# Index projections in a fused attention step: a fifth tile's first feature half placed ahead, the remaining projections one step ahead of the transposes

## The chip, the core and the metric

The kernel runs on one core of a Trainium2 chip. The metric is the device time of one execution in microseconds (us), as a median of several executions. TensorE (PE in the profile) does the matrix products, VectorE (DVE) and ScalarE (ACT) work on tensors, GpSimd (POOL) helps with elementwise work, and SyncE (SP) issues most of the transfers. Each engine takes its own instructions in the order in which they are written; semaphores are the only thing that orders one engine against another.

## The reference, cut to what matters

One layer of a streaming encoder is computed for 1024 prompt tokens and 64 sample tokens, width 1024. The input is normed and modulated to `h`, one combined projection gives everything else, and two attention branches (one that picks its keys by an indexer, one with a sliding window) are gated, merged and added to the input. The part that the change touches is the indexer: its queries `i_q` (4 heads of 64), its key `i_k` (64) and its head weights `i_w` (4), together 324 columns of `h @ w_in`, and the scores made from them.

```python
h = rmsnorm(x, norm_g) * (1 + scale) + shift
p = dict(zip(COL_NAMES, jnp.split(h @ w_in, offs, axis=-1)))
dots = jnp.einsum('nqhd,nkd->nqhk', iq.astype(f32), ik.astype(f32)) * IDX_DIM ** -0.5
score = jnp.einsum('nqhk,nqh->nqk', jax.nn.relu(dots), iw.astype(f32)) * IDX_HEADS ** -0.5
_, sel = lax.top_k(score, k_sel)
```

## The kernel before, in words

The tokens lie in NT = 9 tiles: eight of 128 prompt tokens and one, SAMPLE = 8, of 64. Products in full precision are made from a rounded value and its remainder: `three` issues high times high, high times low and low times high. `HH` and `HL` are the high and low parts of the transposed `h`, 8 blocks of 128 features each; `WH` and `WL` are those of one chunk of the weights.

`project(i, f)` multiplies tile i by the index weights over the feature blocks 4f to 4f+3, that is 12 matmuls of 324 columns, into the PSUM bank `ibank(i)`. Both halves of a tile add up in one bank. Tiles 0 to 3 have banks 0, 1, 4 and 5, and all later tiles have bank 0, so that project(i, 0) of a later tile has to wait (on `idx_evac`) until ScalarE has copied the tile before it out of that bank. `hl_done` counts the parts of `HL` that VectorE has finished. These come in the order of `HORDER`: the first feature half for tokens 0 to 127, 128 to 511 and the rest, then the second feature half in the same three parts.

The first halves of tiles 0 to 3 stand between the last products of the modulation (`ada`). Then comes a loop over i from 0 to ITEMS = 13 in which every engine takes its part:

- TensorE: the projections, then the transposes of item j = i - 1 (L1716, six of them, waiting on `idx_lo`), then the scores of tile j (L1656) for j from 2 to 7, with a piece of the next weight chunk in quarters among the heads. Pieces are the other columns of the combined projection, one tile by 512 columns, 24 matmuls. Piece p is issued at i = p + NAT0, NAT0 = 4. Pieces 0 to 4 all have bank 1 (`pbank`), so piece p waits on `piece_ev` for piece p - 1 to be read out.
- ScalarE: first `nat_evac` of the piece of the iteration before (a copy at L1086 and eight squares with a sum at L1093), then `idx_out(i)`, which copies the projection of tile i to `NIDX` (L1047) and raises `idx_evac`, then the copies of the transposes of item i - 1 to `IQT` (L1117) and `IKT` (L1124), then the relus of the scores (L1078).
- VectorE: `idx_high(i)` makes the rounded part of tile i, then the scores of tile i - 1 are summed up.
- GpSimd: the remainders (L890, L896), which raise `idx_lo`, and for i below 4 one low part of the next chunk's weights (L876).
- SyncE: waits on `idx_evac` for tile i and stores its `i_k` rows (L650, `ik_out`), and for i below 4 a load of raw weights. `NIDX` has two slots, so `idx_out(i)` waits for `ik_out` of tile i - 2, counted on one of two semaphores, and for `idx_lo` of i - 1 items.

After this loop TensorE goes on with the pieces of all remaining chunks, then the attention, then the output projections.

Of the kernel before, what the change touches and what calls it, by code (L numbers as in the profile page):

```python
# [31 lines left out]
NT = SEQ // 128 + 1  # L32
# [15 lines left out]
def rows_of(t):  # L48
    return DEC if t == SAMPLE else 128
# [12 lines left out]
def build_program(nc, t):  # L62

    ctx = ExitStack()
    with ctx:
# [3 lines left out]
        def sem(name):  # L69
            return ctx.enter_context(nc.semaphore(name))  # L70
# [4 lines left out]
        def bank(b):  # L75
            return PS[:, b, :]
# [181 lines left out]
        mod_ready = sem("mod_ready")  # L258
# [9 lines left out]
        idx_evac = sem("idx_evac")  # L268
# [91 lines left out]
        def tcols(tt):  # L360
            return slice(128 * tt, 128 * tt + rows_of(tt))
# [20 lines left out]
        NAT0 = 4  # L382
# [4 lines left out]

        def ibank(i):

            return (0, 1, 4, 5)[i] if i < NAT0 else 0  # L390

        def pbank(p):

# [88 lines left out]
        for q, (_, x) in enumerate(TQ):  # L482
            if x[0] == "P" and unit_keys(x[1]) > 512:
                EV.append("SV"[x[2]])
            else:
                EV.append("V" if EV.count("V") <= EV.count("S") else "S")
# [521 lines left out]
        def _(act):  # L1008
            def w_hi(n):

                c, k = n // KD, n % KD
                if c >= NCH:
                    return
                cw = CHUNKS[c][2]
                if c:
                    act.wait_ge(raw_in[n % 4], 16 * (n // 4 - 1))
                else:
                    act.wait_ge(iraw_in[k // 4], 16)
                if k == 0 and c == 2:
                    act.wait_ge(idx_pe, NT)  # L1020
                if k == 0 and c >= 3:
                    act.wait_ge(piece_pe, PEND[c - 2])
                nc.scalar.activation(WH[c % 2][:, k, 0:cw], RAW[:, n % 4, 0:cw] if c else IRAW[:, k, :], ACT.Copy).then_inc(hi_done, 1)  # L1023
# [16 lines left out]
            def idx_out(i):  # L1040

                r = rows_of(i)
                act.wait_ge(idx_pe, i + 1)
                if i >= 2:
                    act.wait_ge(ik_out[i % 2], 16 * (i // 2))
                    act.wait_ge(idx_lo, i - 1)
                nc.scalar.activation(NIDX[0:r, i % 2, :], bank(ibank(i))[0:r, 0:IDX_W], ACT.Copy).then_inc(idx_evac, 1)  # L1047
# [24 lines left out]
            def relus(tt):  # L1072
                for h in range(4):
                    n = SHEADS.index((tt, h))
                    r, nk = rows_of(tt), keys_of(tt)
                    act.wait_ge(score_pe, n + 1)
                    v = PS[0:r, 4 + 2 * (n % 2):6 + 2 * (n % 2), :].rearrange("p b n -> p (b n)")[:, 0:nk]
                    nc.scalar.activation(v, v, ACT.Relu, scale=HD ** -0.5 * 0.5).then_inc(relu_done, 1)  # L1078

            def nat_evac(c, j, p):  # L1080

                r = rows_of(j)
                dst = STG2[0:r, p % 2, :] if c == 1 else STG[0:r, STG_Q[p] % 3, :]
                if c == 1 and p >= 2:
                    act.wait_ge(stg2_out[p % 2], 16 * (p // 2))
                nc.scalar.activation(dst, bank(pbank(p))[0:r, :], ACT.Copy).then_inc(nat_copied, 1)  # L1086
                act.wait_ge(nat_copied, p + 1)
                blocks = [b for b in range(8) if (8 * (c - 1) + b) % 12 < 10]
                for b in blocks:
                    f = 8 * (c - 1) + b  # L1090
                    head = 10 * (f // 12) + f % 12
                    v = bank(pbank(p))[0:r, HD * b:HD * (b + 1)]
                    last = nc.scalar.activation(v, v, ACT.Square, accum_out=SSQ[0:r, 20 * j + head:20 * j + head + 1])  # L1093
                last.then_inc(piece_ev, 1)

            for i in range(ITEMS + 1):
                if 0 <= i - 1 - NAT0 < NT:
                    act.wait_ge(piece_pe, i - NAT0)
                    nat_evac(1, i - 1 - NAT0, i - 1 - NAT0)
                if 1 <= i < NT:  # L1100
                    idx_out(i)
                if NT <= i < ITEMS:
                    act.wait_ge(idx_t, i - 1)
                    act.wait_ge(cik_in, 16)
                    nc.scalar.activation(IN2[i % 2][:, 4, 0, :], CIK[:, i - NT, :], ACT.Copy)
                    nc.scalar.activation(IN2[i % 2][:, 4, 1, :], CIK[:, i - NT, :], ACT.Copy).then_inc(idx_hi, 1)
                if NT <= i < ITEMS:
                    for n in range(2):
                        w_hi(2 * KD + 2 * (i - NT) + n)
                if i >= 1:  # L1110
                    j = i - 1
                    r = rows_of(j) if j < NT else 128
                    act.wait_ge(idx_t, j + 1)
                    if j == 0:
                        act.wait_ge(hl_done, 24)
                    if j < NT:
                        nc.scalar.activation(IQT[:, :, tcols(j)], bank(2).rearrange("p (h n) -> p h n", h=4)[:, :, 0:r], ACT.Copy)  # L1117
                    if j < SAMPLE:
                        dst = IKT[:, :, tcols(j)]
                    elif j == SAMPLE:  # L1120
                        dst = IKTS[:, :, PAST:PAST + DEC]
                    else:
                        dst = IKTS[:, :, 128 * (j - NT):128 * (j - NT + 1)]
                    nc.scalar.activation(dst, bank(3)[:, 0:256].rearrange("p (h n) -> p h n", h=2)[:, :, 0:r], ACT.Copy).then_inc(idx_tev, 1)  # L1124
                    if 2 <= j < SAMPLE:
                        relus(j)
# [55 lines left out]
            for s in range(S0, S1):  # L1182
# [56 lines left out]
                if s in CACHE_STEP:  # L1239
                    i = CACHE_STEP[s]  # L1240
# [313 lines left out]
        def _(pe):  # L1554
            T = nc.tensor

            def three(out, wh, wl, mh, ml, first, last):

                T.matmul(out, wh, mh, start=first, stop=False)  # L1559
                T.matmul(out, wh, ml, start=False, stop=False)  # L1560
                return T.matmul(out, wl, mh, start=False, stop=last)  # L1561
# [18 lines left out]
            def project(i, f):  # L1580

                r = rows_of(i)
                part = [q for q in range(3) if PARTS[q][1] >= 128 * i + r][0]
                pe.wait_ge(lo_done, 4 * (f + 1))
                pe.wait_ge(hl_done, 12 * f + 4 * part + 4)
                if i >= NAT0:
                    pe.wait_ge(idx_evac, 1 if i == NAT0 else i)
                for k in range(4 * f, 4 * f + 4):
                    last = three(bank(ibank(i))[0:r, 0:IDX_W], HH[:, k, tcols(i)], HL[:, k, tcols(i)],
                                 WH[0][:, k, 0:IDX_W], WL[0][:, k, 0:IDX_W], k == 0, k == KD - 1)  # L1590
                if f == 1:
                    last.then_inc(idx_pe, 1)
# [45 lines left out]
            for i in range(NAT0):  # L1638
                ada(1, 2 * i)
                ada(1, 2 * i + 1)  # L1640
                if i == NAT0 - 1:
                    mod_transposes(1)
                project(i, 0)

            def score_head(tt, h):

# [48 lines left out]
                        piece(p, [h])  # L1695

            for i in range(ITEMS + 1):
                if i == 0:
                    project(0, 1)
                if i + 1 < NAT0:  # L1700
                    project(i + 1, 1)
                if NAT0 <= i < NT:
                    project(i, 0)
                    project(i, 1)
                if i >= 1:
                    j = i - 1
                    r = rows_of(j) if j < NT else 128
                    pe.wait_ge(idx_lo, j + 1)
                    if j >= 1:
                        pe.wait_ge(idx_tev, j)  # L1710
                    slot = IN2[j % 2]
                    for h in range(6):
                        if h < 4 and j >= NT:
                            continue
                        dst = bank(2)[:, 128 * h:128 * h + r] if h < 4 else bank(3)[:, 128 * (h - 4):128 * (h - 4) + r]
                        last = T.transpose(dst.bitcast(F32R), slot[0:r, h, :, :].rearrange("p a d -> p (a d)"), IDR[0:r, 0:r])  # L1716
                    last.then_inc(idx_t, 1)
                    p = i - NAT0 if 0 <= i - NAT0 < NT else None
                    if j == 2:
                        pe.wait_ge(idx_evac, NAT0)  # L1720
                    if 2 <= j < SAMPLE:
                        score(j, p)
                    elif p is not None:
                        piece(p)
# [197 lines left out]
```

## Time and profile before

| what | value |
|---|---|
| median of 3 executions | 1015.71 us (1014.78 to 1016.16) |
| the profiled execution | 1014.79 us |
| its span, first to last instruction | 1013.0 us |
| mean granted clock of TensorE, share of full speed | 0.979 |
| TensorE busy | 953.0 us |
| VectorE busy | 653.4 us |
| ScalarE busy | 393.9 us |
| GpSimd busy | 375.7 us |

In the views a time is in microseconds from the start of the span. In a timeline row the first number is the start of the first instruction of the row, the second how long the row lasted, and what stands in brackets is the idle time of the engine before it with what ended it. A matmul's duration is longer than the distance to the next one, since matmuls overlap; the step from start to start is what a stream of them costs. PEclk is the granted clock, 1.00 for 2.4 GHz and 0.50 for 1.2 GHz.

### The profile page before, as it was taken

The page shows a single profiled execution, that of the slowest core. Times are in us where ns is not written, and L with a number is a line of the kernel's source. Part 1 is how long each engine was busy: PE and PEld are TensorE (multiplying, and loading weights), DVE is VectorE, ACT ScalarE, POOL GpSimd, SP SyncE. Part 2 cuts the span into 40 slices and gives each one's busy share as a digit, 9 for nine tenths or more (in the row PEclk, how much of TensorE's full clock was granted, in tenths as well). Part 3 has the DMA queues.
Part 4 walks back from the last instruction along what each step waited for, and adds up shares of the span by engine and source line. Part 5 has one row for each costly group of instructions (what it writes and reads, how often), then busy time and mean ns, then how long its engine had stood idle before and what let it go on. Part 6 is the DMA issues. An engine that isn't in the chain of part 4 may idle for free.

```text
span 1013.0 us, 17631 instructions
## 1 busy us (share of the span) xinstructions
PE 953.0 (94%) x6468; PEld 851.8 (84%) x6482; DVE 653.4 (65%) x1375; ACT 393.9 (39%) x1166; POOL 375.7 (37%) x420
## 2 busy tenths in 40 slices
PE   3859999999999999999999889999999879999998
PEld 2558887878789999999999767778867769999998
DVE  6563365999999999999980477665665543331111
ACT  5674566444322322122211566666655522212100
POOL 0261123222243533121233488655640325527332
PEclk9989999999999999999999799999999989999999
DMA  9830013643461323232132755433246475534242
GB/s 322 304 78 25 24 46 107 225 154 102 140 202 60 115 82 108 80 108 76 63 136 70 236 147 145 122 92 86 83 129 174 108 232 152 153 98 135 97 124 73
DMA packets 113243, 126.92 MB, mean 125 GB/s; under 512 B 13161, under 2 KB 90361, under 8 KB 113034
## 3 DMA queue, kind: packets, MB, share of 16 engines
q1 hardware_dynamic: 102754, 114.82, 36.5%
q10 hardware_dynamic: 10408, 11.01, 3.5%
q8 instruction: 52, 0.85, 0.4%
q14 instruction: 29, 0.24, 0.1%
HBM read 95.75 MB, written 36.02 MB: 130 GB/s over the span
## 4 chain that ended last, share of the span: by engine, by line
PE 81%; issue 5%; POOL 4%; DVE 3%; ACT 3%; DMA 3%; SPq 1%; ACTq 0%; POOLq 0%; DVEq 0%
PE PS L1559 20%; PE PS L1560 20%; PE PS L1561 20%; PE PS L1801 6%; PE PS L1827 5%; PE PS L1742 4%; PE PS L1656 2%; PE PS L1760 1%; PE PS L1805 1%; POOL YO L1004 1%; PE PS L1620 1%; DMA XN<-in_x_prompt 1%; DMA ZST<-attd 1%; PE PS L1568 1%; DVE HL L1338 1%
## 5 line engine op out<-in xcount | busy, mean ns | idle before, releaser
L1559 PE MATMUL PS<-HH,WH 128*128 128x384 f32 (+1 forms) x576 | 188.8, 328 | 0.0
L1561 PE MATMUL PS<-HH,WL 128*128 128x384 f32 (+1 forms) x576 | 187.9, 326 | 0.0
L1560 PE MATMUL PS<-HL,WH 128*128 128x384 f32 (+1 forms) x576 | 187.7, 326 | 0.0
L1394 DVE MAX8 M<-SC 128x8 f32<-128x384 f32 (+3 forms) x210 | 174.7, 870 | 11.6 <-DVE SC L1399 11.0
L1399 DVE MATCH_REPLACE8 SC<-M,SC 128x384 f32<-128x384 f32 (+3 forms) x210 | 179.9, 863 | 0.0
L876 POOL TENSOR_TENSOR WL<-RAW,WH 128x512 fp32r<-128x512 f32 x72 | 94.2, 1312 | 180.8 <-ACT WH L1023 180.8
L1559 PE MATMUL PS<-WH,HH 128*128 128x512 f32 (+3 forms) x288 | 110.2, 382 | 8.9 <-DVE HL L1338 8.7
L1559 PEld LDWEIGHTS PS<-HH,WH 128*128 128x128 f32 x576 | 108.1, 188 | 3.8 <-issue 3.7
L1560 PE MATMUL PS<-WL,HH 128*128 128x512 f32 (+3 forms) x288 | 108.3, 376 | 0.0
L1561 PE MATMUL PS<-WH,HL 128*128 128x512 f32 (+3 forms) x288 | 108.2, 376 | 0.0
L1560 PEld LDWEIGHTS PS<-HL,WH 128*128 128x128 f32 x576 | 108.1, 188 | 0.0
L1561 PEld LDWEIGHTS PS<-HH,WL 128*128 128x128 f32 x576 | 108.1, 188 | 0.0
L1221 ACT ACTIVATE PB<-PB,NM 128x256 f32<-128x256 f32 (+9 forms) x136 | 86.2, 634 | 25.1 <-DVE NM L1495 24.0
L1150 ACT ACTIVATE STG<-PS 128x384 f32<-128x384 f32 (+1 forms) x48 | 22.8, 475 | 155.1 <-PE PS L1561 155.1
L1559 PE MATMUL PS<-UH,MH 128*128 128x256 f32 (+1 forms) x288 | 81.5, 283 | 0.0
L1560 PE MATMUL PS<-UL,MH 128*128 128x256 f32 (+1 forms) x288 | 81.4, 283 | 0.0
L1561 PE MATMUL PS<-UH,ML 128*128 128x256 f32 (+1 forms) x288 | 81.2, 282 | 0.0
L1559 PE MATMUL PS<-ZH,WOH 128*128 128x384 f32 (+1 forms) x192 | 63.9, 333 | 9.0 <-DVE TM L1538 5.7
L1549 DVE TENSOR_TENSOR YT<-PS,GATE 128x256 f32<-128x256 f32 (+1 forms) x36 | 15.3, 424 | 87.0 <-PE PS L1561 71.2
L1559 PEld LDWEIGHTS PS<-WH,HH 128*128 128x128 f32 (+1 forms) x288 | 53.8, 187 | 20.0 <-POOL WL L876 8.8
L1495 DVE CUSTOM_DVE_ANT_0 PB<-PS,BTA 128x256 f32<-128x256 f32 (+6 forms) x56 | 46.1, 823 | 33.5 <-PE PS L1805 21.9
L1742 PE MATMUL PS<-IDF,PB 128*128 128x128 f32 (+1 forms) x436 | 65.4, 279 | 0.1
(202 smaller groups left out, 1957.0 us busy)
## 6 DMA issues: line engine op xcount, KB each, us to landing
RAW<-in_w_all SPq DMA_DIRECT2D x72, 256.0 KB, 2.7
gz<-STG SPq DMA_DIRECT2D x48, 192.0 KB, 1.8
WADA<-in_w_ada SPq DMA_DIRECT2D x16, 512.0 KB, 11.9
snat<-STG SPq DMA_DIRECT2D x24, 256.0 KB, 2.0
QKV<-snat SPq DMA_DIRECT2D x8, 768.0 KB, 5.8
GT<-gz SPq DMA_DIRECT2D x32, 192.0 KB, 2.5
XN<-in_x_prompt SPq DMA_DIRECT2D x8, 512.0 KB, 6.6
btad<-bvd ACTq DMA_DIRECT2D x4, 1024.0 KB
```

Of the source, the lines that this page charges most:

```text
L876: nc.gpsimd.tensor_tensor(WL[c % 2][:, k, 0:cw], raw, WH[c % 2][:, k, 0:cw].bitcast(F32), ALU.subtract).then_inc(lo_done, 1)
L1150: nc.scalar.activation(STG[:, q % 3, 0:gn], bank(pbank(p))[:, 0:gn], ACT.Sigmoid).then_inc(piece_ev, 1)
L1221: nc.scalar.activation(PB[u % NPB][0:r, 0:nk], PB[u % NPB][0:r, 0:nk], ACT.Exp, scale=-1.0, bias=NM[0:r, br, h:h + 1], accum_out=DEN[0:r, ...
L1394: V.max(M8[0:r, a, :], w).then_inc(sel_step, 1)
L1399: V.match_replace(w, M8[0:r, a, :], w, TAKEN).then_inc(sel_step, 1)
L1495: V.tensor_tensor_reduce(out=PB[u % NPB][0:r, 0:nk], in0=v, in1=bias, scale=1.0, scalar=init, op0=ALU.add, op1=ALU.min, accum_out=NM[0:r, ...
L1559: T.matmul(out, wh, mh, start=first, stop=False)
L1560: T.matmul(out, wh, ml, start=False, stop=False)
L1561: return T.matmul(out, wl, mh, start=False, stop=last)
L1742: last = T.transpose(out[0:m, c:c + r], PB[v % NPB][0:r, 128 * b:128 * b + m], IDF[0:r, 0:r])
L1801: last = T.matmul(out, q, keys[:, kv, part, k0 + b:k0 + b + m], start=(part == 0), stop=(part == 1 and br == 1))
L1827: last = T.matmul(PS[half, 7, 128 * h:128 * h + r], v, PT[PSLOT[u + kv] % 3][0:m, p_col(u + kv, b):p_col(u + kv, b) + r], start=(b == 0), ...
```

## The change

Tile 4 gets a bank of its own, bank 6. Its first feature half is issued right after that of tile 3, before the loop; its second half is issued in the loop at i = 2. The second halves of tiles 1, 2 and 3 are spread otherwise (0 and 1 at i = 0, 2 and 3 at i = 1). Tiles 5 to 8, which were projected at the iteration of their own number, are now projected one iteration earlier, at i = 4 to 7, so that there is no projection at i = 8. ScalarE copies tile 4 out at i = 3, after tile 3; the others keep their places on ScalarE. The first score waits for five copies rather than four. No instruction is added or removed.

```diff
         def ibank(i):
 
-            return (0, 1, 4, 5)[i] if i < NAT0 else 0
+            return (0, 1, 4, 5, 6)[i] if i <= NAT0 else 0
...
-                if 1 <= i < NT:
+                if 1 <= i < NT and i != NAT0:
                     idx_out(i)
+                if i == NAT0 - 1:
+                    idx_out(NAT0)
...
                 pe.wait_ge(hl_done, 12 * f + 4 * part + 4)
-                if i >= NAT0:
-                    pe.wait_ge(idx_evac, 1 if i == NAT0 else i)
+                if i == NAT0:
+                    pe.wait_ge(mod_ready, 1)
+                if i > NAT0 and f == 0:
+                    pe.wait_ge(idx_evac, 1 if i == NAT0 + 1 else i)
...
                 project(i, 0)
+            project(NAT0, 0)
...
-                if i == 0:
-                    project(0, 1)
-                if i + 1 < NAT0:
-                    project(i + 1, 1)
-                if NAT0 <= i < NT:
-                    project(i, 0)
-                    project(i, 1)
+                for n in {0: (0, 1), 1: (2, 3), 2: (4,)}.get(i, ()):
+                    project(n, 1)
+                if NAT0 <= i < NT - 1:
+                    project(i + 1, 0)
+                    project(i + 1, 1)
...
                     if j == 2:
-                        pe.wait_ge(idx_evac, NAT0)
+                        pe.wait_ge(idx_evac, NAT0 + 1)
```

## Rows read from the trace of the kernel before

**Rows 1.** The page: chain that ended last, by engine.
```profile
PE 81%; issue 5%; POOL 4%; DVE 3%; ACT 3%; DMA 3%; SPq 1%; ACTq 0%; POOLq 0%; DVEq 0%
```
**Rows 2.** Busy time by stretch (busy us and instructions of each engine, PEclk, DMA).
```profile
45.00:84.00 39.00, 27.30 (x170) 23.65 (x169) 22.49 (x46) 23.16 (x52) 20.48 (x25) 0.82 0.25 62
84.00:145.00 61.00, 60.85 (x325) 52.04 (x324) 24.42 (x41) 32.97 (x121) 6.36 (x16) 1.00 0.07 25
145.00:560.00 415.00, 414.09 (x2357) 382.23 (x2356) 363.82 (x660) 125.33 (x479) 127.01 (x118) 1.00 0.35 114
```
**Rows 3.** Timeline of TensorE, 52 to 83 us: projections, transposes (L1716), first scores.
```profile
52.95 0.38 PE L1559 MATMUL PS<-WH,HH 128*128 128x324 f32 x1 [0.90 <-DVE HL L1338]
...
59.34 0.46 PE L1559 MATMUL PS<-WH,HH 128*128 128x324 f32 x1 [4.37 <-DVE HL L1338]
...
69.66 0.96 PE L1716 MATMUL PS<-IDR,IN 128*128 128x128 f32 x6 [2.69 <-POOL IN L896]
72.18 1.00 PE L1716 MATMUL PS<-IDR,IN 128*128 128x128 f32 x6 [1.56 <-POOL IN L896]
74.24 1.62 PE L1656 MATMUL PS<-IKT,IQT 128*128 128x384 f32 x4 [1.05 <-ACT IKT L1124]
...
77.98 0.47 PE L1559 MATMUL PS<-WH,HH 128*128 128x324 f32 x1
...
82.47 0.63 PE L1716 MATMUL PS<-IDR,IN 128*128 128x128 f32 x6
```
**Rows 4.** Timeline of VectorE: the last `HL`, all of `hl_done`.
```profile
66.86 0.76 DVE L1338 TENSOR_TENSOR HL<-XT,HH 128x576 fp32r<-128x576 f32 x1 [0.34 <-ACT HH L1068]
```
**Rows 5.** Timeline of ScalarE, 71 to 74 us: tile 3 out, then the transposes' copies.
```profile
71.41 0.45 ACT L1047 ACTIVATE NIDX<-PS 128x324 f32<-128x324 f32 x1
73.22 0.60 ACT L1117 ACTIVATE IQT<-PS 128x512 fp32r<-128x512 f32 x1 [1.36 <-PE PS L1716]
73.72 0.38 ACT L1124 ACTIVATE IKT<-PS 128x256 fp32r<-128x256 f32 x1
```
**Rows 6.** SyncE, 70 to 80 us: tile 2's store issued; landing times of both stores there.
```profile
71.29 0.43 SPq L650 DMA_DIRECT2D out_pa_ik<-NIDX  x1
...
DMA to landing us min/median/max: 2.6/2.6/2.6
```
**Rows 7.** Timeline of TensorE, end of piece 0, tile 5's projection, transposes, piece 1.
```profile
90.07 0.39 PE L1561 MATMUL PS<-WH,HL 128*128 128x512 f32 x1
90.30 0.31 PE L1559 MATMUL PS<-WH,HH 128*128 128x324 f32 x1
...
93.88 0.62 PE L1716 MATMUL PS<-IDR,IN 128*128 128x128 f32 x6
94.34 0.47 PE L1559 MATMUL PS<-WH,HH 128*128 128x512 f32 x1
```
**Rows 8.** Timeline of ScalarE beside it: piece 0 read out (8 squares), then tile 5.
```profile
90.50 0.60 ACT L1086 ACTIVATE STG<-PS 128x512 f32<-128x512 f32 x1 [0.78 <-PE PS L1561]
...
92.67 0.21 ACT L1093 ACTIVATION_READ_ACCUMULATOR PS<-PS 128x1 f32 x1
94.08 0.44 ACT L1047 ACTIVATE NIDX<-PS 128x324 f32<-128x324 f32 x1 [1.20 <-PE PS L1561]
```
**Rows 9.** Timeline of TensorE at i = 8: tile 8's projection (24 matmuls), transposes.
```profile
128.38 0.31 PE L1559 MATMUL PS<-WH,HH 128*64 128x324 f32 x1
...
131.91 0.63 PE L1716 MATMUL PS<-IDR,IN 128*128 128x128 f32 x6
```
**Rows 10.** Timeline of ScalarE at i = 8: the copy of piece 3.
```profile
128.58 0.60 ACT L1086 ACTIVATE STG<-PS 128x512 f32<-128x512 f32 x1 [0.48 <-PE PS L1561]
```
**Rows 11.** Busy time by stretch of 1 us, around the falls and rises of the clock, and one long wait.
```profile
59.00:60.00 1.00, 0.66 (x3) 0.69 (x4) 1.00 (x2) 0.03 (x1) 1.00 (x1) 0.76 0.67 158
...
69.00:70.00 1.00, 0.34 (x3) 0.35 (x4) 0.74 (x3) 0.00 (x0) 1.00 (x4) 0.88 0.00 0
...
585.00:586.00 1.00, 0.00 (x0) 0.00 (x0) 1.00 (x3) 0.73 (x3) 1.00 (x1) 1.00 0.04 11
```

## The prediction

> **What bounds the kernel now.** First I read the chain that ended last: 81% of it is TensorE [rows 1]. Then I cut the span into stretches. From 84 to 145 us, the part of the loop that has pieces, TensorE is busy for 60.85 of 61 us, and from 145 to 560 us for 414.09 of 415 [rows 2]. The reader is to see that there is no slack on TensorE from 84 us on: whatever TensorE loses or saves there moves the end by the same amount. Before 84 us it is otherwise: 27.30 of 39 us are busy, at a mean clock of 0.82 [rows 2]. The timeline of TensorE shows the holes: 0.90 and 4.37 us in wait for the low parts of `h`, 2.69 and 1.56 us in wait for GpSimd's remainders, 1.05 us in wait for ScalarE's copies [rows 3]. Last I read ScalarE's timeline around one full iteration of the loop, since two of its copies decide when PSUM banks 0 and 1 are free.
>
> **The change part by part.** The matmuls are the same ones; only their places and waits differ.
>
> *Tile 4's first half ahead.* It is 12 matmuls. A projection at full clock takes 93.88 - 90.30 = 3.58 us for 24 [rows 7], so half of one is 1.8 us. Tile 3's first half ends where the hole of 0.90 us begins, at 52.05, so this one ends at about 53.9. It waits for the third part of `HL`'s first half, which VectorE makes before the part that project(0, 1) waits for at 52.95, and for the modulation, older still. It pushes project(0, 1), 12 matmuls, from 52.95 to about 53.9, and that ends near 55.7 instead of 54.8. Behind it lies the hole of 4.37 us that VectorE ends at 59.34 [rows 3]. Cost 0; if that hole were not there, 1.8.
>
> *Second halves regrouped, tile 4's at i = 2.* project(3, 1) now goes ahead of the transposes of item 0, which therefore end near 66.9 rather than 65.0. ScalarE and VectorE are at work on the last part of `h` until 67.6 [rows 4], and their copies come after it, so nobody waits. project(4, 1) needs the last `HL`, done at 66.86 + 0.76 = 67.62 [rows 4]. It runs to about 69.5, and the next transposes start at 69.66, when GpSimd lets them [rows 3]. It just fits in the hole of 2.69 us. Cost 0; at half clock it would run 1.5 us over, but the transposes behind are bound by GpSimd again at 72.18, so that this too would be hidden.
>
> *ScalarE copies tile 4 at i = 3.* This copy has a new neighbour: it stands ahead of the copies of item 2's transposes, and it waits for the store of tile 2's keys, since both use the same slot of `NIDX`. SyncE issues that store at 71.29, behind its load of raw weights, and the landing takes 2.6 us [rows 6], so 73.89; the copy takes 0.45 [rows 5], so 74.3. In the kernel before, the copies behind it start at 73.22 [rows 5], and the first score at 74.24 waits for them [rows 3]. What is queued behind the waiting copy is `IQT` and `IKT`, and who waits for those is TensorE. Cost +1.1 us. If the store landed before 72.8 it would be 0; these are the two bounds.
>
> *Tile 5 in place of tile 4 at i = 4.* Same place, same 24 matmuls, bank 0 long free. Cost 0. It took 82.47 - 77.98 = 4.5 us because its first part ran at half clock [rows 3].
>
> *Tiles 6, 7, 8 at i = 5, 6, 7.* Here is the term that decides. Before, the projection of tile i at iteration i needed the copy of tile i - 1, done an iteration ago. Now iteration 5 opens with project(6, 0), and that needs the copy of tile 5. ScalarE makes this copy at its own iteration 5, but behind `nat_evac` of piece 0, and piece 0 is what TensorE has only just ended. So TensorE's stream stops. The working from the rows: the last matmul of piece 0 starts at 90.07 and the next instruction at 90.30 [rows 7]; ScalarE starts the copy of the piece at 90.50, and ends the last of the eight squares at 92.88 [rows 8]. The copy of tile 5 would follow with some 0.1 us of overlap, as neighbours on ScalarE have, and 0.44 long [rows 8]: 92.76 to 93.2. From the end of a copy on ScalarE to TensorE's start goes 0.14 us (`IKT` ends 74.10, the score starts 74.24) [rows 3, 5]. So project(6, 0) starts at 93.34 instead of 90.30: a stall of 3.04 us. Before, the projection covered this reading out: it and the transposes fill 90.30 to 94.34 [rows 7], and piece 1 finds its bank free. Tiles 7 and 8 have the same stall. Cost 3 x 3.04 = +9.1 us. Bounds: 2.9 to 3.2 each.
>
> *Iteration 8 without a projection.* The 24 matmuls of tile 8 took 131.91 - 128.38 = 3.53 us [rows 9]; these go. But they covered the reading out of piece 3, which begins at 128.58 [rows 10]. Now the transposes (0.46 us, as 94.34 - 93.88 [rows 7]) come first, and piece 4 waits for its bank 1 until 2.38 + 0.20 + 0.14 = 2.72 us after the end of piece 3. That leaves 2.26 us idle. Cost -3.53 + 2.26 = -1.3 us. ScalarE's copies for the first head come before the piece's first quarter is over, so the score doesn't wait further.
>
> *The sum at the clock of before.* 0 + 0 + 1.1 + 0 + 9.1 - 1.3 = +8.9 us.
>
> **The clock.** After the 4.37 us wait the granted clock goes to half within 59 to 60 us; after the 2.69 us wait at about 69.8 [rows 3, 11]. But at 585 us a wait of over 2 us leaves it at 1.00 [rows 11]. My stalls of 3.04 us lie between, so a fall after one of them can go either way. What one costs: 24 matmuls took 4.5 us where they began at half clock against 3.58 at full [rows 3, 7], that is 0.9, and as 12 matmuls at half clock from 59.34 take 3.2 against 1.8 us, up to 1.5. I take one fall of 1.5 among the four stalls. The bounds are -0.9 (none, and the half clock at 77.98 gone too, since project(4, 1) now fills the hole before the fall at 69.8) and +6 (all four). The Trainium skill (TensorE: Matmul & The Clock Gate, section "HAM oscillation — how this bites in real kernels") says that bursts of matmuls with waits between them can throttle the clock anew at each repetition. The row at 585 us speaks against it for a wait of this size and the one at 69.8 us for it; by the rule the sum would be the second rival's.
>
> **The value.** +8.9 + 1.5 = +10.4 us. The profiled execution took 1014.79 and would take 1025.2; the median shown is 0.92 above it, so the forecast is 1026.1 us, a factor of 1.010. Bounds: the least is 8.7 + 0 - 1.3 - 0.9 = +6.5 (1022.2), the most 9.6 + 1.2 - 1.3 + 6 = +15.5 (1031.2), to which a half microsecond of spread between executions is added.
>
> **The rivals.**
>
> *The copies are ready in time (faster).* If tile 5's copy did not in fact lie behind the piece's reading out for TensorE, only the moved projection would count: -3.53 for iteration 8, +2.26 for its bank, +1.1 for the late copy: -0.2 without and, if piece 4's wait were hidden as well, -2.4 us, 1013.3. It would take that the copy of the tile ends before the piece does. It decides where the reading out starts: the rows have it start 0.20 us after the piece's end, not before [rows 7, 8], and ScalarE's order is fixed. For it speaks only that the three holes before 84 us are real. Faster: 3 in 100. Between the two, no change that can be measured: 3 in 100.
>
> *The clock falls after each stall (slower still).* Four falls of 1.5 us on top of 8.9 give +14.9, 1030.6 us. For it: the fall after 2.69 us of waiting [rows 3, 11]. Against: 585 us [rows 11], and that 9 us of dense work lie between two stalls. 17 in 100.
>
> *The stalls are given back later.* VectorE's choice of keys, which runs beside the pieces, begins later, and TensorE has its own waits from 560 us on. If these waits were for something that doesn't depend on TensorE, part of the 8.9 would vanish there, say half: +4.5, 1020.2 us. Against: in 145 to 560 us TensorE is busy without a hole [rows 2], and what it waits for later is made from its own results. 7 in 100.
>
> **How the numbers follow.** The forecast (stalls as worked out, none to two falls) has 70 in 100: 1022 to 1029. The four-fall case adds 17, the given-back case 7, and 6 are left for faster or same. The range 1021.0 to 1031.5 takes in the first two, with the bounds, and leaves out the rest. About 0.2%, or 2 us, is what a measurement of this kernel can tell from no change. Faster 0.03, same 0.03, slower 0.94.
>
> **What would show it.** In the changed kernel's timeline of TensorE there should be three holes of about 3.0 us after the last quarters of pieces 0, 1 and 2, each ended by ScalarE's `NIDX` (L1047), and one of about 2.3 us after the transposes of item 7, ended by the squares at L1093. The waits of 2.69 us at 66.9 should shrink to about 0.9 and a small one. The first score should start near 75.3 instead of 74.24, with ScalarE's `NIDX` ahead of it at 73.9. The stretch from the first score to the end of iteration 8 should be longer by some 8 to 9 us, and all after it as long as before. I am wrong if the holes are ended sooner than ScalarE's eight squares, or if the clock row shows 0.50 in several iterations.

## The result, and the profile after

The changed kernel takes 1028.79 us (median of 4, 1027.61 to 1030.52) against 1015.25 for the kernel before in the same rounds: 1.0127 times, interval 1.0109 to 1.0144. Measured once more later (run r1_change, below), it was 1.0156 times, 1.0137 to 1.0174. It is slower by 13 to 16 us. The profiled execution of the first measurement took 1030.52 us, its span is 1028.7, its mean granted clock 0.970 (before: 0.979).

First the waits of TensorE over the whole span: line waited for, total us, times, the longest.

```profile
PE PS L1561 <- ACT NIDX L1047: 8.7, 3, 2.9
PE PS L1561 <- DVE HL L1340: 7.0, 2, 3.7
...
PE PS L1661 <- ACT IKT L1126: 3.7, 1, 3.7
...
PE PS L1561 <- ACT PS L1093: 2.0, 1, 2.0
```

The first and the last of these did not exist before. The reader is to see that the three waits in the first line are equal (2.89 us each) and that it is `NIDX`, the copy of an index projection, that ends them. In the timeline of TensorE they are here (piece 0 ends, tile 6's projection begins; then tiles 7 and 8; then piece 4):

```profile
94.27 0.39 PE L1563 MATMUL PS<-WH,HL 128*128 128x512 f32 x1
97.55 0.39 PE L1561 MATMUL PS<-WH,HH 128*128 128x324 f32 x1 [2.89 <-ACT NIDX L1047]
...
102.71 0.63 PE L1719 MATMUL PS<-IDR,IN 128*128 128x128 f32 x6
...
114.52 0.38 PE L1561 MATMUL PS<-WH,HH 128*128 128x324 f32 x1 [2.89 <-ACT NIDX L1047]
118.12 0.64 PE L1719 MATMUL PS<-IDR,IN 128*128 128x128 f32 x6
...
130.15 0.51 PE L1561 MATMUL PS<-WH,HH 128*64 128x324 f32 x1 [2.89 <-ACT NIDX L1047]
135.08 0.62 PE L1719 MATMUL PS<-IDR,IN 128*128 128x128 f32 x6
...
147.27 0.50 PE L1561 MATMUL PS<-WH,HH 128*128 128x512 f32 x1 [2.00 <-ACT PS L1093]
```

In the kernel before the projection begins 0.23 us after the last matmul of the piece [rows 7]; here it begins 3.28 us after it, so the stream has lost 3.05 us (the bracket counts from the last matmul's modelled end and so has 0.16 less). Beside it ScalarE reads out the piece and only then the tile:

```profile
94.70 0.60 ACT L1086 ACTIVATE STG<-PS 128x512 f32<-128x512 f32 x1 [0.78 <-PE PS L1563]
95.33 0.21 ACT L1093 ACTIVATE PS<-PS 128x64 f32<-128x64 f32 x1
...
96.86 0.21 ACT L1093 ACTIVATION_READ_ACCUMULATOR PS<-PS 128x1 f32 x1
96.92 0.49 ACT L1047 ACTIVATE NIDX<-PS 128x324 f32<-128x324 f32 x1
```

Before the first score, ScalarE waits for a transfer, and TensorE for ScalarE (ScalarE's timeline, then TensorE's):

```profile
76.08 0.44 ACT L1047 ACTIVATE NIDX<-PS 128x324 f32<-128x324 f32 x1 [3.70 <-DMA out_pa_ik<-NIDX]
```
```profile
77.42 1.62 PE L1661 MATMUL PS<-IKT,IQT 128*128 128x384 f32 x4 [3.72 <-ACT IKT L1126]
```

Last the clock. The columns are those of rows 2: busy time by stretch; the third number from the right is PEclk, here 1.00, then 0.51 and 0.50.

```profile
98.00:99.00 1.00, 1.00 (x9) 1.00 (x8) 0.04 (x1) 0.00 (x0) 0.89 (x2) 1.00 0.15 33
99.00:100.00 1.00, 1.00 (x6) 1.00 (x5) 0.00 (x0) 0.00 (x0) 0.41 (x2) 0.51 0.00 0
100.00:101.00 1.00, 1.00 (x5) 1.00 (x5) 0.00 (x0) 0.00 (x0) 0.00 (x0) 0.50 0.00 0
```

TensorE resumes at 97.55 at full clock and falls to 1.2 GHz at about 99.0, when it is busy again. The 24 matmuls of tile 6 take 102.71 - 97.55 = 5.16 us instead of 3.58 [rows 7]. The hole before tile 7 had no fall behind it: its 24 matmuls take 118.12 - 114.52 = 3.60 us. The fall that belongs to the third hole comes inside it, at about 129.7, while TensorE is idle until 130.15:

```profile
129.00:130.00 1.00, 0.00 (x0) 0.00 (x0) 0.00 (x0) 1.00 (x8) 0.00 (x0) 0.87 0.44 164
130.00:131.00 1.00, 0.85 (x4) 0.75 (x5) 0.50 (x3) 0.01 (x1) 0.29 (x1) 0.50 0.10 22
```

Tile 8 then takes 135.08 - 130.15 = 4.93 us instead of 3.53 [rows 9].

To compare kernels I cut each span at four marks: the start of project(1, 1), where the 3.7 to 4.4 us wait for `HL` ends; the first score; the transposes of item 8; and the end. Times in us, from the profiled executions:

| kernel | mark 1 to first score | first score to item 8 | item 8 to end |
|---|---|---|---|
| before | 14.90 | 67.85 | 870.9 |
| changed | 17.34 | 79.61 | 871.7 |
| changed, once more | 15.99 | 81.95 | 870.5 |

The middle column holds most of the loss: 11.8 and 14.1 us. The spans differ by 15.7 us in both traces, and the rest is 2.4 and 1.1 us on the way to the first score, 0.7 and 1.0 ahead of mark 1 (which comes at 58.4 to 60.3 us in the traces of all kernels, so this is spread), and 0.8 and -0.5 in the last stretch. In the first 418 us behind item 8, TensorE is busy for 417.09 us before and 417.10 after, so nothing is given back there.

### The profile page after: what moved, and what is told of

It reads as the page before. It is cut to its first block, busy times and chain, and to the rows that moved or that the text cites. A ratio compares the mean times of both kernels' runs of the same rounds, so it can differ in the third digit from the quotient of the medians.

```text
span 1028.7 us, 17645 instructions
## 1 busy us (share of the span) xinstructions
PE 961.8 (93%) x6482; PEld 857.0 (83%) x6482; DVE 650.7 (63%) x1375; ACT 392.8 (38%) x1166; POOL 376.1 (37%) x420
## 4 chain that ended last, share of the span: by engine, by line
PE 78%; issue 5%; POOL 4%; DMA 4%; ACT 3%; DVE 2%; SPq 1%; ACTq 0%; POOLq 0%; DVEq 0%
PE PS L1561 19%; PE PS L1563 19%; PE PS L1562 19%; PE PS L1804 5%; PE PS L1830 5%; PE PS L1745 4%; PE PS L1661 2%; PE PS L1808 1%; PE PS L1763 1%; POOL YO L1004 1%; DMA XN<-in_x_prompt 1%; PE PS L1624 1%; ACT PS L1093 1%; DMA ZST<-attd 1%; PE PS L1570 1%
## 5 line engine op out<-in xcount | busy, mean ns | idle before, releaser
L1561 PE MATMUL PS<-WH,HH 128*128 128x512 f32 (+3 forms) x288 | 112.4, 390 | 18.7 <-ACT NIDX L1047 8.7
L1551 DVE TENSOR_TENSOR YT<-PS,GATE 128x256 f32<-128x256 f32 (+1 forms) x36 | 15.3, 424 | 86.9 <-PE PS L1563 71.8
```

## The experiments

**The copy ahead of the piece (e1_copy_first).**

```diff
+                if NAT0 < i < NT:
+                    idx_out(i)
                 if 0 <= i - 1 - NAT0 < NT:
                     act.wait_ge(piece_pe, i - NAT0)
                     nat_evac(1, i - 1 - NAT0, i - 1 - NAT0)
-                if 1 <= i < NT and i != NAT0:
+                if 1 <= i < NAT0:
                     idx_out(i)
```

> The changed kernel with one order turned round on ScalarE: from iteration 5 on, the index projection of tile i is copied out before the finished piece is read out, not behind it. Theory (the three projections of tiles 6 to 8 wait for a copy queued behind the piece): the three holes of 2.89 us ended by NIDX go, and with them the two stretches of half clock that followed; the hole before piece 4 stays, 0.3 to 0.5 us longer at most. So 8.7 + about 3 us less than the changed kernel, some 1017 us. Rival (the projections wait for something else of the piece, such as its bank or ScalarE being busy as such): the holes stay or move to the piece behind, 1026 us or more.

Measured: 1017.5 us, 1.0018 times the kernel before (1.0005 to 1.003). By the two ratios, one turned order on ScalarE takes back 11 of the 13 us. In its trace no wait of TensorE is ended by `NIDX` any more; the waits from 50 to 170 us begin with these:

```profile
PE PS L1563 <- DVE HL L1342: 3.8, 1, 3.8
PE PS L1663 <- ACT IKT L1128: 2.2, 1, 2.2
PE PS L1563 <- ACT PS L1093: 2.0, 1, 2.0
```

The stretch from first score to item 8 is 68.55 us instead of 79.61. The rival falls: the projections waited for the copy's place in ScalarE's order, and with that mended TensorE begins each of them without a pause.

**Tile 4 ahead alone (e3_tile4_only).** The loop of the changed kernel with tiles 5 to 8 back at their own iterations:

```diff
-                if NAT0 <= i < NT - 1:
-                    project(i + 1, 0)
-                    project(i + 1, 1)
+                if NAT0 < i < NT:
+                    project(i, 0)
+                    project(i, 1)
```

> The first part of the change alone: tile 4 has bank 6, its first half is ahead and its second at i = 2, but tiles 5 to 8 are projected at the iteration of their own number as in the kernel before. Theory: no hole ended by NIDX in iterations 5 to 7 and none before piece 4; the projection at i = 4 is gone from the dense part (4.5 us less there), the first score is still 2 to 2.5 us later, because ScalarE's copy of tile 4 waits for a store. So 1 to 3 us faster than before, 1012.5 to 1014.5 us. Rival (moving tile 4 ahead is itself what costs, by delaying the transposes): slower than before.

Measured: 1015.76 us, 0.9997 times (0.9984 to 1.0011), no difference; I had expected 1 to 3 us. No hole ended by `NIDX` is there, as expected. But the first score is 0.92 us later after mark 1 (15.82 against 14.90; I had expected 2 to 2.5), and the way from it to item 8 is only 2.69 us shorter (65.16), not 4.5: TensorE's clock is at half from 71.8 to 82.0 us (69.8 to 79.9 before), although tile 4's projection is gone from there, and the next matmuls, those of piece 0, ran in the slow time in its place. The clock in this trace, then in the trace before:

```profile
81.00:82.00 1.00, 1.00 (x4) 0.81 (x3) 0.00 (x0) 0.00 (x0) 0.40 (x2) 0.50 0.00 0
82.00:83.00 1.00, 1.00 (x5) 0.83 (x5) 0.06 (x1) 0.67 (x2) 0.00 (x0) 0.98 0.00 0
```
```profile
79.00:80.00 1.00, 1.00 (x5) 1.00 (x5) 0.46 (x2) 0.00 (x0) 0.00 (x0) 0.50 0.00 0
80.00:81.00 1.00, 1.00 (x9) 1.00 (x8) 0.00 (x0) 0.00 (x0) 0.00 (x0) 1.00 0.00 0
```
From the transposes of item 3 to those of item 4 it takes 91.19 - 77.94 = 13.25 us here and 93.88 - 82.47 = 11.41 before [rows 3, 7]. So the step that took 4.5 us in the row was worth 4.5 less the 1.8 by which its neighbours grew, 2.7 us.

**One step ahead alone (e4_step_only).** The kernel before, with

```diff
-                if NAT0 <= i < NT:
-                    project(i, 0)
-                    project(i, 1)
+                if NAT0 - 1 <= i < NT - 1:
+                    project(i + 1, 0)
+                    project(i + 1, 1)
```

> The second part alone: all projections one step ahead of the transposes, tile 4's whole projection at i = 3 in bank 0, nothing of it earlier and no bank 6. Theory: the three holes of 2.9 us in iterations 5 to 7 and that of 2.0 us before piece 4 are there as in the changed kernel, a smaller one of about 1 us at i = 4; the store's wait isn't. Part of tile 4's projection lies in the hole before the transposes of item 2. So 8 to 12 us slower than before, 1023 to 1027 us. Rival (the loss comes from the wait for the store): about as before.

Measured: 1032.23 us, 1.0168 times (1.0144 to 1.0191). Every hole that was expected is there, 9.7 us by `NIDX` in four:

```profile
PE PS L1559 <- ACT NIDX L1047: 9.7, 4, 2.9
...
PE PS L1559 <- ACT PS L1093: 2.0, 1, 2.0
```

I had expected 1023 to 1027 us, so the size was off by 5 us and more. Tile 4's projection at i = 3 pushes the first score back by 2.8 us (17.70 against 14.90), more than I had allowed, and the clock fell at two of the holes. The rival falls too: the wait for the store is not there, and the loss is. The second part of the change alone is thus as bad as the whole or worse; the first part doesn't cause the loss.

**Tile 4 ahead in bank 7 (e5_tile4_bank7).** As e3_tile4_only, and

```diff
-            return (0, 1, 4, 5, 6)[i] if i <= NAT0 else 0
+            return (0, 1, 4, 5, 7)[i] if i <= NAT0 else 0
...
-                if 1 <= i < NT and i != NAT0:
+                if 1 <= i < NT:
                     idx_out(i)
-                if i == NAT0 - 1:
-                    idx_out(NAT0)
...
-                    pe.wait_ge(mod_ready, 1)
+                    pe.wait_ge(mod_ready, 2)
...
-                        pe.wait_ge(idx_evac, NAT0 + 1)
+                        pe.wait_ge(idx_evac, NAT0)
+                    if j == 4:
+                        pe.wait_ge(idx_evac, NAT0 + 1)
```

> As the run with tile 4 alone ahead, but tile 4 lies in bank 7, which no score needs until tile 4's own, so that ScalarE copies it at i = 4 as in the kernel before and the first score waits neither for the copy nor for the store. Theory: the first score starts as in the kernel before, near 74.3 to 75, and one projection of 3.6 to 4.5 us is gone from the dense part: 3.5 to 4.5 us faster than before, about 1011 us. Rival (the late first score has another cause, such as the transposes coming later): no better than with bank 6.

Measured: 1012.57 us, 0.9965 times (0.9953 to 0.9977). This beats the kernel before by 3.7 us. It was expected at about 1011 us. Against e3_tile4_only, measured in the same rounds, it is 3.2 us lower in the medians; the traces show 1.6 us of that from mark 1 to item 8 (79.37 against 80.98), and the rest is not explained. Before the first score there is the wait of 1.05 us of before, none for the store, so the rival falls:

```profile
74.24 1.35 PE L1659 MATMUL PS<-IKT,IQT 128*128 128x384 f32 x4 [1.05 <-ACT IKT L1124]
```

**The holes filled (e7_filled, r3_filled).** The changed kernel with extra matmuls whose result nobody reads:

```diff
+                if NAT0 < i < NT - 1:
+                    for _ in range(12):
+                        T.matmul(bank(3), HH[:, 0, 0:128], HH[:, 0, 0:512], start=True, stop=True)
```

> The changed kernel with each of the three holes filled: 12 matmuls of 512 columns into a bank that is free, some 2.8 us, stand ahead of the projections of tiles 6, 7 and 8, at the place where TensorE waited 2.89 us for the copy. TensorE's place in the schedule stays, only its idleness goes. Theory (part of the loss is the clock, which fell after two of the holes and made the 24 matmuls behind take 5.2 and 4.9 us instead of 3.6): no half clock between 95 and 150 us except perhaps before piece 4, and 1 to 3 us less than the changed kernel, 1026 to 1028 us. Rival (the clock costs nothing in the median, falls being rare): the same time as the changed kernel, 1028.8, or a little more.

Measured: 1027.4 us, 1.0116 times (1.0089 to 1.0143). The matmuls take the place of the waiting almost exactly, and the clock stays:

```profile
92.03 2.88 PE L1707 MATMUL PS<-HH 128*128 128x512 f32 x12
95.09 0.38 PE L1561 MATMUL PS<-WH,HH 128*128 128x324 f32 x1 [0.18 <-ACT NIDX L1047]
```
```profile
95.00:96.00 1.00, 0.91 (x6) 0.94 (x7) 0.50 (x3) 0.00 (x0) 0.34 (x1) 1.00 0.14 30
96.00:97.00 1.00, 1.00 (x9) 1.00 (x8) 0.00 (x0) 0.00 (x0) 0.96 (x3) 1.00 0.02 3
```

Tile 6's projection takes 98.70 - 95.09 = 3.61 us in it. The median is 1.4 us under that of the changed kernel, which was taken in other rounds; that can't be told from nothing, so by the median alone the rival stands.

**Bank 7 within the changed kernel (e2_bank7, r2_bank7).** The edit of e5_tile4_bank7 on the changed kernel.

> The changed kernel with tile 4 in bank 7 and its copy at i = 4, so that the first score waits neither for this copy nor for the store of tile 2's keys. All else as in the changed kernel. Theory: the wait of 3.72 us before the first score is 1.05 again, the first score is 2.2 to 2.7 us earlier than in the changed kernel, the holes of 2.89 us stay. So 2 to 3 us less than the changed kernel, 1026 to 1027 us. Rival (the wait is hidden or moves on): 1028.8 us.

Measured: 1030.09 us, 1.0139 times (1.0114 to 1.0163), where I had expected 1026 to 1027: not lower than the changed kernel's first measurement, as the rival had it. Yet its first score comes 14.80 us after mark 1, as in the kernel before, and 2.5 sooner than in the changed kernel's trace. So I measured the three together, in the same rounds.

> The changed kernel once more, on the same chip and in the same rounds as the next two. All theories: 1.011 to 1.014 times the kernel before. Its first score should start about 1.0 us later after project(1, 1) than in the kernel before if the landing of 4.0 us in its first trace was a chance, 2.4 us if it belongs to the change.

> Tile 4 in bank 7 and its copy at i = 4 within the changed kernel, once more, since its first median was no lower than the changed kernel's, taken on another occasion. Theory (the wait for the store costs 1 to 2.4 us in the first scores, and what hid the gain was the spread of the clock in the attention, from 840 us of the span's start back to 570): 1 to 2 us less than the changed kernel in the same rounds. Rival (taking the wait away lets the clock fall after all three holes, or its gain is lost for good): the same as the changed kernel.

> The three holes filled with matmuls, once more in the same rounds as the changed kernel. Theory (the clock falls after about two of three holes, 1.5 us each): 2 to 3 us less than the changed kernel. Rival (falls are rare in the median): no less.

| kernel | median us | ratio to before | mark 1 to first score | first score to item 8 | item 8 to end |
|---|---|---|---|---|---|
| r1_change | 1031.06 | 1.0156 (1.0137 to 1.0174) | 15.99 | 81.95 | 870.5 |
| r2_bank7 | 1029.99 | 1.0135 (1.0114 to 1.0155) | 14.68 | 82.26 | 870.8 |
| r3_filled | 1028.52 | 1.0119 (1.0098 to 1.014) | 15.93 | 76.89 | 876.1 |

The ratio of r1_change lies above the 1.011 to 1.014 that I expected for it. Its first score comes 1.09 us later after mark 1 than before, which is the case in which the landing of 4.0 us in the first trace was a chance. The other two medians are 1.1 and 2.5 us under the changed kernel's, both as the theories had it, but the intervals of the three overlap, so the medians alone don't show either gain. The traces show where it would come from. Bank 7 takes 1.31 us off the way to the first score and has 0.3 us more behind it. In r1_change the clock fell behind each of the three holes and behind that of piece 4. The three, from the timeline of TensorE:

```profile
95.45 0.39 PE L1561 MATMUL PS<-WH,HH 128*128 128x324 f32 x1 [2.89 <-ACT NIDX L1047]
100.62 0.62 PE L1719 MATMUL PS<-IDR,IN 128*128 128x128 f32 x6
...
112.40 0.39 PE L1561 MATMUL PS<-WH,HH 128*128 128x324 f32 x1 [2.88 <-ACT NIDX L1047]
117.59 0.62 PE L1719 MATMUL PS<-IDR,IN 128*128 128x128 f32 x6
...
129.59 0.33 PE L1561 MATMUL PS<-WH,HH 128*64 128x324 f32 x1 [2.88 <-ACT NIDX L1047]
134.70 0.63 PE L1719 MATMUL PS<-IDR,IN 128*128 128x128 f32 x6
```

Each projection takes 5.1 to 5.2 us instead of 3.5 to 3.6, so a fall costs 1.6 here (1.58 and 1.40 in the changed kernel's first trace). With the holes filled, the stretch from first score to item 8 is 81.95 - 76.89 = 5.1 us shorter, which is three falls (4.8) and little else. In that one execution of r3_filled the last stretch was 5.6 us longer than in r1_change, with 39.1 us at half clock in it against 31.8, so the spans came out equal. My estimate from these two numbers: 7.3 us more at half the clock cost at most 3.7 us, so the clock is not all of the 5.6, and the rest isn't explained.

**All three waits taken away (e10_piece4_bank0).** The edits of e1_copy_first and of bank 7 together on the changed kernel, and

```diff
-            return (1, 1, 1, 1, 1, 0, 1, 0, 1)[p] if p < NT else (p - 7) % 4
+            return (1, 1, 1, 1, 0, 1, 0, 1, 0)[p] if p < NT else (p - 7) % 4
```

with the waits of pieces 4, 5 and 11 set to match.

> The whole change with all three of its waits taken away: tile 4 in bank 7, the tile copied out ahead of the piece on ScalarE, and piece 4 in bank 0 (pieces 5 to 8 in banks 1, 0, 1, 0), so that it needn't wait for piece 3 to be read out. Theory: no hole of over 1 us between 84 and 145 us, and the work of TensorE there is that of the run with tile 4 alone in bank 7, so the same time as that, 1011 to 1013 us, 3 to 5 us faster than before. Rival (projecting a step ahead costs in itself): 1015 us or more.

Measured: 1015.28 us, 0.9991 times (0.9973 to 1.0009), not the 1011 to 1013 that I expected. The trace shows a new hole of 1.31 us, at the first head of iteration 8 (TensorE, then ScalarE beside it):

```profile
129.88 0.39 PE L1563 MATMUL PS<-WH,HL 128*128 128x512 f32 x1
131.58 2.11 PE L1661 MATMUL PS<-IKT,IQT 128*128 128x512 f32 x8 [1.31 <-ACT IKT L1126]
```
```profile
130.41 0.27 ACT L1093 ACTIVATE PS<-PS 128x64 f32<-128x64 f32 x1
...
130.61 0.65 ACT L1119 ACTIVATE IQT<-PS 128x512 fp32r<-128x512 f32 x1
131.09 0.44 ACT L1126 ACTIVATE IKT<-PS 128x256 fp32r<-128x256 f32 x1
```

Piece 4 now starts at once, and its first quarter is over before ScalarE, which is reading out piece 3, gets to the copies of the transposes. The wait has only moved from the piece to the head: from first score to item 8 it takes 66.17 us, 1.5 more than e5_tile4_bank7. This hole does not explain the median, though. The ten executions lie in two groups, four from 1011.58 to 1012.85 and six from 1015.23 to 1016.84, and the traced one, hole and all, took 1011.88, which is in the faster group and in the range that I expected. What parts the groups stays open, and so the rival (that projecting a step ahead costs in itself, 1015 us or more) stands for the median; in the trace only the hole speaks for it.

**Tile 5 among the first scores (e9_tile5_in_scores).** On top of the last kernel, project(5) is taken from i = 4 and split by two feature blocks each:

```diff
+                    if tt == 2 and h == 0:
+                        pe.wait_ge(idx_evac, 1)
+                        project_part(NAT0 + 1, 0)
                     if h == 0:
...
                     if p is not None and h >= 1:
                         piece(p, [h])
+                    if tt == 2 and h >= 1:
+                        project_part(NAT0 + 1, h)
```

> As the run with all three waits taken away, and tile 5's projection is moved too, from i = 4 into the first scores at i = 3, six matmuls before the first head and six after each of the other three, where TensorE waits for ScalarE and VectorE. Theory: the holes of 1.05 and 0.58 us there and part of the half clock are used, and the projection of 3.6 to 4.5 us at i = 4 is gone, while the scores end 2 to 3 us later: 1 to 2 us less than the run without it, about 1010.5 us. Rival (the first scores are the critical chain and the matmuls among them delay it by all they take): the same time or more.

Measured: 1008.85 us, 0.9939 times (0.9919 to 0.9959), 6.1 us under the kernel before and the fastest kernel of this study. From mark 1 to item 8 it takes 77.99 us, 80.84 without this step and 82.75 in the kernel before. The one of 1.3 us in iteration 8 is still there; the holes of 1.05 and 0.58 us among the first heads are gone, and the rival falls:

```profile
73.94 1.65 PE L1670 MATMUL PS<-IKT,IQT 128*128 128x384 f32 x4
77.00 0.60 PE L1670 MATMUL PS<-IKT,IQT 128*128 128x384 f32 x2
78.33 0.51 PE L1670 MATMUL PS<-IKT,IQT 128*128 128x384 f32 x2
79.56 0.64 PE L1733 MATMUL PS<-IDR,IN 128*128 128x128 f32 x6
```

I had expected 1 to 2 us less than without this step. The two traced executions differ by 3.7 us, of which 2.9 lie between mark 1 and item 8 and 1.1 in the last stretch. The medians differ by 6.4 us, since most executions of e10_piece4_bank0 lie in its slower group; what of that belongs to this step is not shown.

## Why the prediction was right, and where it was off

The direction, the place and the mechanism were right, and 1028.8 lies in the range of 1021.0 to 1031.5; the later measurement of 1031.06 just does. The value of 1026.1 was too low by 2.7 to 5 us. Step by step:

- *Tile 4's first half ahead, and the second halves regrouped, cost 0*: held. The transposes of item 2 follow mark 1 by 12.92 us (73.00 - 60.08) and by 12.84 before (72.18 - 59.34) [rows 3]. project(4, 1) filled the hole of 2.69 us.
- *The copy of tile 4 waits for the store, +1.1*: held in most traces, +1.09 in r1_change and +1.04 in e1_copy_first. In the first trace it was +2.44, since the store took 4.0 us to land where the row before had 2.6 [rows 6]. My upper bound of 1.2 took one landing for all.
- *Tile 5 in place of tile 4, cost 0*: +0.99 in the first trace and +0.06 in r1_change, from the first score to the transposes of item 3. Tile 4's projection did fill the hole of 2.69 us, but the half clock at the first scores did not go, as my lower bound had it: it lasted to 85.2 us (79.9 before).
- *Three stalls of 3.04 us*: 3.05 each. ScalarE's order was the cause (e1_copy_first).
- *Iteration 8, -3.53 + 2.26*: the hole was 2.00 us by the bracket, 2.16 of the stream.
- *The clock, one fall of 1.5 us*: this term was mis-sized. A fall costs 1.4 to 1.6 us, as I had it, but there were two at the holes in the first trace, three in e2_bank7's, and four in r1_change and r2_bank7, counting that behind piece 4. Without a fall the sum for the median would have been 1024.6. The sign of being wrong that I had named, a clock row of 0.50 in several iterations, did come: in two of the four with a hole in the first trace and in all four in r1_change. So the place and the size of the stalls were right by working, and the median lies in the range because the range had room for the falls.

Summed for the first trace, from first score to item 8: 3 x 3.05 + 2.16 - 3.53 = 7.78, falls of 1.58 and 1.40, and 0.99 for the scores and tile 5's projection, whose half clock lasted longer (9.22 us from first score to the transposes of item 3 against 8.23): 11.75, measured 11.76.

Of the rivals, the one with a fall behind each stall gave 1030.6 at 17 in 100. It is what r1_change showed, in its trace and its median. I had weighed one wait of over 2 us without a fall at 585 us [rows 11] against one fall at 69.8 us, and gave the first too much weight. In the timeline of TensorE before, it is a wait of 2.44 us:

```profile
586.49 0.27 PE L1746 MATMUL PS<-IDF,RDEN 128*8 128x128 f32 x1 [2.44 <-DVE RDEN L1517]
```

My stalls of 3.04 us do not lie between the two, as I wrote: they are longer than both, and the waits of 2.69 and 4.37 us both had a fall. Length alone doesn't decide it either, since one of the three equal holes in the first trace had none. The section of the Trainium skill named there ("HAM oscillation — how this bites in real kernels", in TensorE: Matmul & The Clock Gate) says that bursts with waits between them can throttle the clock anew each time. The traces agree in part: r1_change has it four times in a row and the changed kernel's first trace at two of four holes, and r3_filled, with no idle stretch before the projections, has none there. The rival of copies ready in time would have needed ScalarE's other order, which is what e1_copy_first gives. Nothing is seen to be given back later: item 8 to end is 870.9 before and 870.5 to 871.7 after, in traces that differ by up to 7 us there among all kernels.

## What to carry to other kernels

Moving work ahead on one engine moves what it waits for ahead as well: before an instruction is put a step earlier, look at what stands in front of its releaser in the other engine's order, since a projection that covered a read-out became one that waits for it. Where a buffer is shared, the copy that frees it goes ahead of longer work that nobody waits for yet. And a step taken out of a slow-clock stretch is worth the time in its row less what its neighbours then lose: 4.5 - 1.8 us in e3_tile4_only.

## What the runs showed that I had not expected

The clock often falls only after a hole, when TensorE is busy again: it resumed at 97.55 us at full clock and fell to half at about 99.0, and in r1_change it fell about 0.4 us after resuming at 95.45. But it also falls inside one: 0.4 us before TensorE resumed at 130.15 in the first trace, and 0.2 us before it resumed at 127.99 in e4_step_only. Holes of 2.9 us had a fall, inside them or within 1.5 us behind them, in 2 of 3 cases in the changed kernel's first trace and in e4_step_only, and in 3 of 3 in r1_change, r2_bank7 and e2_bank7. The hole of 2.0 us, with six short transposes ahead of it, was followed by one in r1_change, r2_bank7, r3_filled and e1_copy_first, and by none in the first trace, e2_bank7, e4_step_only and e7_filled.

The last stretch, item 8 to end, has the same instructions in all kernels and took 869.1 to 876.1 us in the traces. TensorE's time at half clock in it was 25 us in the kernel before (870.9), 35 in e9_tile5_in_scores (869.1) and 39 in r3_filled (876.1), so the time at half clock does not order them, and what makes the spread stays open.
